# Projections ordered by mixer group, loads that wait for their own group's stores, and attention woven in from inside the first projection

## The chip, the cores and the metric

The kernel runs on one core of a Trainium2 chip. The metric is the device time of one execution in microseconds (us). The engines are called as in the profile: PE is TensorE (matmuls), PEld its weight loads, DVE is VectorE, ACT is ScalarE, POOL is GpSimd, SP is SyncE.

## The reference

One inference step of a two-layer encoder (model width 1024) for two request groups: a prompt of 1024 new frames, and 32 next frames of a running stream with 512 cached ones. All is float32. In each layer:

```python
u = rmsnorm(x, norm1) @ w_in          # one projection, its columns cut into
# A: aq, ak, av (6 heads)   B: bq, bk, bv (5 heads), index iq, ik, iw   C: cq, cf, ci, cg (5 heads)
oa = diff_attend(aq, ak, av)          # softmax(q1 k1) - lam * softmax(q2 k2), chunk-causal
ob = dsa_attend(bq, iq, iw, bk, bv, ik)   # keys picked by top-256 of an index score, then softmax
oc = hgrn2(cq, cf, ci)                # gated linear recurrence
x = x + concat(rms(oa), ob, rms(oc) * silu(cg)) @ w_out
x = x + (silu(conv3(h @ up_a)) * (h @ up_g)) @ w_down      # h = rmsnorm(x, norm2)
```

Rotated keys, values, index keys, the recurrence's states and the convolution's tails are outputs too.

## The kernel before, in words

**Passes.** The 1056 frames are cut into two halves: half 0 is the first 512 prompt frames and the 32 running ones (544 columns, in column groups of 272 and 272), half 1 the other 512 (groups of 256). A layer and a half are a pass, and `PROJS` numbers them: pass 0 is layer 0, half 0; pass 1 is layer 0, half 1; passes 2 and 3 the same in layer 1.

**Dense work** is a list of 974 turns (`TURNS`), in stages in this order: P00, P01, F00, P10, F01, P11, F10, Y0, F11, Y1, where P is a projection, F the output projection with the FFN, Y the last norm, and the digits are layer and half. A turn is one accumulated group of matmuls, eight as a rule, and each of them leaves two records in the trace, so a turn has 16. The kinds:
- `f`: one 128-row tile of the transposed projection (weights stationary, L650). 19 tiles `n`, two column groups `j` each. Two tiles x = 0, 1 make a bundle of mixer B (n 0 to 7) or A (n 8 to 13), whose halves POOL rotates (rotary embedding); each of n 14 to 18 is a bundle of mixer C. ScalarE evicts the turn into `ub` (L917), POOL rotates into `tb` (L1540 to L1545), SP stores to `projT` in HBM. Both buffers hold two bundles.
- `t`: values and gates with frames as rows (frames stationary, L658), six chunks `p` of 224 weight columns. A chunk has one turn for each unit of 128 frames (and one for the 32 running ones), so five in half 0 and four in half 1. Evicted into `tout` (two buffers, L923), stored to `projN`.
- `wo`, `a`, `g`, `dn`: output projection, the FFN's two up-projections and its down-projection, all on L650. `nsq` and `nsc`: a norm's mean by matmul (L627) of squares that ScalarE makes (L899), then ScalarE's square root (L904), VectorE's reciprocal and its products `xn`.

In numbers of turns P00 is 0 to 71 and P01 72 to 137. Weights come through a ring of three tiles; SP loads a tile when the third before it is done. On SP's one queue stand, in the order of turns, the weight loads, the bundles' stores (taken up four turns after a bundle's last turn) and the `t` stores (one turn after).

**Mixer work** is a list of steps: per pass X (index scores and picks, steps `load`, `dots`, `near`, `far`, `pick`), B (attention of mixers B and A: a load step, one step for each item and three to drain), C (HGRN2: three head pairs of ten steps), M (merge). An item is one head and one unit of frames. Its scores (L713 for B, L728 for A) go to PSUM; VectorE masks and takes maxima (L1313 for B), ScalarE takes exponentials (L1038), VectorE scales them (L1324), TensorE transposes (L744), ScalarE copies (L1050), TensorE multiplies by values (L761, L768), ScalarE copies out (L1061, L1064). In C, step 7 makes products of pairs (L795), which VectorE masks and sums and ScalarE copies (L1137), and step 8 uses them (L863, L864).

**The order of both** is written out ahead of time. `weave` gives one string of "d" (next dense turn) and "s" (next step), and PE, ACT and DVE all follow it. A step may not stand before its turn `first`. For X that is turn 5's tile plus LAG = 6; for B, C and M it is the end of the pass's whole projection plus 6:

```python
first = LAST["f", l, h, 5, 0] + 1 + LAG if kind == "X" else STAGE["P%d%d" % (l, h)][1] + LAG
while j < len(steps) and i >= steps[j][0] and y / need <= (x + time / 2) / have:
```

Steps are shared out by their estimated times: `y` counts step time given out and `x` dense time passed, and when `first` is late, all steps that are due by then come at once. That happens in pass 0, where turns 22 to 137 (P00 and P01) share X, B, C and M of pass 0: X ends behind turn 53, and behind turn 77 stand 37 steps of B in a row; the other 22 stand behind turns 78 to 93. In pass 2 the same 59 steps are spread behind turns 428 to 487 in F01. In the scalar engine's program (`att_scalar`) the B part begins with a wait for all stores of the pass's projection, and then `load_pair` issues the loads of the first two head pairs (7 DMAs each in half 0).

## Time and profile before

| | |
|---|---|
| median of three runs | 4173.93 us (4170.97 to 4179.95) |
| the profiled execution's own time | 4175.74 us |
| its span, first to last instruction | 4173.9 us |
| mean granted TensorE clock | 0.945 |
| TensorE busy | 3863.0 us (93%) |
| VectorE, ScalarE, POOL busy | 54%, 26%, 15% |
| HBM traffic | 80 GB/s over the span |

Busy time of PE is the union of pipelined matmuls, so it says whether the engine had work and not how fast it went; the granted clock tells which of its two levels, 1.2 or 2.4 GHz, it had, as a mean over a stretch (0.5 is all at 1.2 GHz). The page cuts the span into 40 slices of 104 us and gives busy shares and the granted clock in tenths. A row of the timeline gives an instruction or several merged ones with start and duration, and in brackets the idle time of the engine before it and what ended it. Line numbers are those of the kernel before.

### The profile page before, as it was taken

The numbers are of one execution on the slowest core, as the hardware profiler recorded it, in microseconds if no ns is written. First come the engines' busy times: TensorE is split into PE (matmuls) and PEld (weight loads), VectorE is DVE, ScalarE is ACT, GpSimd is POOL, SyncE is SP. The second block draws the span as 40 slices with busy tenths as digits, with TensorE's granted clock in tenths as the row PEclk, the third lists the DMA queues.
The fourth block names the chain that finished last, engine by engine and source line by source line (L and its number), as shares of the span: only waits on it lengthen the run. The fifth ranks groups of instructions, "written<-read, shape, count | busy, mean of one in ns | idle before, by whom it ended". The sixth has DMA issues, their size and how long they took to land.

```text
span 4173.9 us, 54852 instructions
## 1 busy us (share of the span) xinstructions
PE 3863.0 (93%) x22040; PEld 3134.7 (75%) x22040; DVE 2243.5 (54%) x4588; ACT 1083.9 (26%) x2674; POOL 645.0 (15%) x732
## 2 busy tenths in 40 slices
PE   7996889999999999999999998999999999799997
PEld 6773667877876777887767776897767777688886
DVE  1744654599954564449555553489835564521112
ACT  1113333211124342221333232111144433211111
POOL 3200230211001133020000014302000101421013
PEclk9995898999999999999999999999999998899999
DMA  3321222322122122232221113333211211332222
GB/s 129 116 77 59 62 69 89 107 86 71 55 85 66 57 85 88 89 111 91 77 87 54 59 56 105 109 115 104 67 57 54 74 39 57 103 121 71 71 75 93
DMA packets 152565, 338.04 MB, mean 81 GB/s; under 512 B 30312, under 2 KB 70760, under 8 KB 141048
## 3 DMA queue, kind: packets, MB, share of 16 engines
q1 hardware_dynamic: 91800, 289.52, 22.1%
q10 hardware_dynamic: 60512, 45.02, 3.8%
q8 instruction: 175, 2.87, 0.3%
q14 instruction: 78, 0.64, 0.1%
HBM read 298.34 MB, written 36.14 MB: 80 GB/s over the span
## 4 chain that ended last, share of the span: by engine, by line
PE 71%; DVE 18%; DMA 3%; ACT 3%; ACTq 2%; issue 2%; POOL 1%; SPq 0%; DVEq 0%; POOLq 0%
PE PS L650 48%; PE PS L658 7%; DVE scr L1285 5%; DVE top L1284 4%; PE PS L744 3%; PE PS L728 3%; PE PS L768 2%; PE PS L761 2%; PE PS L713 1%; DMA out_projT<-dense 1%; PE PS L864 1%; PE PS L863 1%; PE PS L795 1%; DVE xn L1231 1%; DMA iw<-out_projT 1%
## 5 line engine op out<-in xcount | busy, mean ns | idle before, releaser
L650 PE MATMUL PS<-xn,wring 128*128 128x272 f32 (+1 forms) x8064 | 1883.3, 394 | 48.1 <-ACT dense L940 19.9
L650 PEld LDWEIGHTS PS<-xn,wring 128*128 128x128 f32 x8064 | 1551.8, 194 | 335.3 <-issue 38.8
L1512 POOL TENSOR_TENSOR xT<-xT,res 128x272 f32<-128x272 f32 (+1 forms) x320 | 254.2, 795 | 2810.6 <-ACT res L909 2765.4
L650 PE MATMUL PS<-dense,wring 128*128 128x256 f32 (+1 forms) x2816 | 668.5, 396 | 16.3 <-ACT res L909 7.9
L650 PEld LDWEIGHTS PS<-dense,wring 128*128 128x128 f32 x2816 | 540.9, 195 | 116.9 <-issue 14.3
L1284 DVE MAX8 top<-scr 128x8 f32<-128x384 f32 (+6 forms) x418 | 367.5, 879 | 12.5
L1285 DVE MATCH_REPLACE8 scr<-top,scr 128x384 f32<-128x384 f32 (+6 forms) x418 | 359.8, 861 | 0.0
L658 PE MATMUL PS<-wring,xn 128*128 128x224 f32 (+1 forms) x1728 | 352.2, 365 | 6.0 <-ACT dense L923 6.0
L658 PEld LDWEIGHTS PS<-wring,xn 128*128 128x128 f32 (+1 forms) x1728 | 319.1, 188 | 32.0 <-issue 9.5
L909 ACT ACTIVATE res<-PS 128x272 f32<-128x272 f32 (+1 forms) x320 | 124.2, 389 | 640.5 <-PE PS L650 617.8
L650 PE MATMUL PS<-catT,wring 128*128 128x272 f32 (+1 forms) x1024 | 235.5, 392 | 7.5 <-DMA wring<-in_wo 6.9
L650 PEld LDWEIGHTS PS<-catT,wring 128*128 128x128 f32 x1024 | 196.4, 193 | 46.2 <-DMA wring<-in_wo 7.3
L744 PE MATMUL PS<-ident,scr 128*128 128x128 f32 (+1 forms) x902 | 165.9, 294 | 63.3 <-ACT scr L1050 44.6
L744 PEld LDWEIGHTS PS<-ident,scr 128*128 128x128 f32 (+1 forms) x902 | 104.5, 151 | 155.2 <-issue 54.7
L1313 DVE CUSTOM_DVE_ANT_0 scr<-PS,bias 128x128 f32<-128x128 f32 (+8 forms) x90 | 67.7, 753 | 255.9 <-PE PS L744 235.9
L938 ACT ACTIVATE dense<-PS 128x256 f32<-128x256 f32 (+1 forms) x176 | 68.6, 391 | 475.8 <-PE PS L650 468.2
L1050 ACT ACTIVATE scr<-PS 128x512 f32<-128x512 f32 (+4 forms) x308 | 139.1, 452 | 186.3 <-PE PS L744 133.1
L1303 DVE MEMSET PS<- 64x64 f32 x192 | 21.5, 112 | 308.1 <-PE PS L728 307.6
L1305 DVE TENSOR_REDUCE mx<-PS 128x1 f32<-128x640 f32 (+6 forms) x216 | 162.5, 752 | 31.8 <-PE PS L728 25.3
L917 ACT ACTIVATE dense<-PS 128x256 f32<-128x256 f32 (+1 forms) x152 | 58.6, 389 | 444.3 <-PE PS L650 330.7
L1038 ACT ACTIVATE scr<-PS,ngm 128x640 f32<-128x640 f32 (+6 forms) x216 | 157.4, 731 | 43.2 <-DVE ngm L1306 42.7
L728 PE MATMUL PS<-kv 32*128 32x512 f32 (+5 forms) x672 | 140.0, 524 | 23.5 <-ACT scr L1038 20.2
(172 smaller groups left out, 3343.1 us busy)
## 6 DMA issues: line engine op xcount, KB each, us to landing
wring<-in_wu SPq DMA_DIRECT2D x88, 1024.0 KB, 4.9
wring<-in_wf SPq DMA_DIRECT2D x76, 512.0 KB, 3.8
wring<-in_wo SPq DMA_DIRECT2D x64, 512.0 KB, 3.6
wring<-in_wd SPq DMA_DIRECT2D x96, 320.0 KB, 2.9
wring<-in_wd SPq DMA_DIRECT2D x64, 384.0 KB, 3.1
wring<-in_wn SPq DMA_DIRECT2D x24, 896.0 KB, 5.0
kv<-out_projT ACTq DMA_DIRECT2D x48, 256.0 KB, 3.9
out_projN<-dense SPq DMA_DIRECT2D x96, 112.0 KB, 1.7
```

The lines of the kernel that those rows point to most:

```text
L650: mm = nc.tensor.matmul(PS[:, dbank(t.g0), 0:cw], wtile(t.q, i), rhs, start=(kk == a), stop=(kk == b - 1))
L658: mm = nc.tensor.matmul(PS[:u.w, dbank(t.g0), 0:CW], xn[:, kk, u.col:u.col + u.w], wtile(t.q, kk, CW), start=(kk == 0), stop=(kk == KD - 1))
L728: mm = nc.tensor.matmul(PS[:u.w, abank(s, u, x) + a // 512, 0:b - a], q[r, u.col:u.col + u.w], k[r, u.key + a:u.key + b], start=True, stop ...
L744: tr = nc.tensor.transpose(PS[:kw, 4, (kt % 4) * P:(kt % 4) * P + u.w], soft(s, 0)[:u.w, kt * P:kt * P + kw], ident[:u.w, :u.w])
L761: mm = nc.tensor.matmul(PS[r0:r0 + D, 5, 0:u.w], v[:kw, u.vt + kt, D * it.hh:D * it.hh + D], pt_of(it)[:kw, kt, 0:u.w], start=(kt == 0), s ...
L909: nc.scalar.activation(res[:, i % NRES, 0:cw], PS[:, dbank(t.g0), 0:cw], ACT.Copy).then_inc(s_ea, 1)
L1038: nc.scalar.activation(dst, src, ACT.Exp, bias=ngm[:u.w, s % 4, x:x + 1], scale=scale_a if g == "a" else 1.0, accum_out=sums[:u.w, s % 4, ...
L1050: nc.scalar.activation(pt_of(items[s])[:kw, 4 * z:4 * z + n, 0:u.w], src[:, :, 0:u.w], ACT.Copy).then_inc(s_pc, 1)
L1284: step(nc.vector.max(top[:u.w, :], wk))
L1285: step(nc.vector.match_replace(wk, top[:u.w, :], wk, SENTINEL))
L1305: step(nc.vector.tensor_reduce(mx[:u.w, i, x:x + 1], sc, AX, ALU.max))
L1512: nc.gpsimd.tensor_tensor(x, x, res[:, i % NRES, 0:cw], ALU.add).then_inc(s_res, 1)
```

## The change

- `SECTIONS` orders the turns of each projection by mixer: section b is f tiles 0 to 7 and then t chunks 1, 2, 3; section a is f tiles 8 to 13 and chunk 0; section c is f tiles 14 to 18 and chunks 4, 5. Turns and their number are the same.
- Each `load_pair` waits for the stores of its own section and those before it, in place of one wait for all.
- `weave` lets a B step start six turns after the end of the section whose loads it needs (`step_groups`), and C and M after section c. Shares are counted as a running credit.
- The squares of tiles 5 to 7 of a layer-0 norm go to a free part of `cat`, since `catT` 5 to 7 may hold attention's output by then.

```diff
--- before.py
+++ after.py
@@ -59,6 +59,8 @@
 C_AV, C_BV, C_CI, C_CG, WN = 0, 384, 704, 1024, 1344
 NCH, CW = 6, 224
 
+SECTIONS = (("b", 8, (1, 2, 3)), ("a", 14, (0,)), ("c", NPT, (4, 5)))
+
 P_N1, P_N2, P_CONV, P_HIST, P_AG, P_CG, P_LI, PCOLS = 0, 8, 16, 104, 148, 212, 276, 278
 
 LEVELS = (64, 32, 16, 8, 4, 2)
@@ -93,13 +95,17 @@
 
     if l == 0:
         _norm(l, h, 0, 0, 1)
-    for n, j in ((0, 0), (1, 0), (2, 0), (0, 1), (1, 1), (2, 1)) + tuple((n, j) for n in range(3, NPT) for j in range(2)):
-        _turn("f", l, h, n, 0, j, load=("f", l, h, n, 0))
-        if (n, j) == (0, 0):
-            _norm(l, h, 0, 1, 1 - l)
-    for p in range(NCH):
-        for u in UNITS[h]:
-            _turn("t", l, h, u.slot, p, load=("t", l, h, 0, p))
+    order = ((0, 0), (1, 0), (2, 0), (0, 1), (1, 1), (2, 1)) + tuple((n, j) for n in range(3, NPT) for j in range(2))
+    done = 0
+    for g, end, chunks in SECTIONS:
+        for n, j in order[2 * done:2 * end]:
+            _turn("f", l, h, n, 0, j, load=("f", l, h, n, 0))
+            if (n, j) == (0, 0):
+                _norm(l, h, 0, 1, 1 - l)
+        for p in chunks:
+            for u in UNITS[h]:
+                _turn("t", l, h, u.slot, p, load=("t", l, h, 0, p))
+        done = end
 
 
 def _added(kind, l, h, p, norm):
@@ -155,6 +161,17 @@
 
 ADDS = {k: i for i, k in enumerate([k for k, t in enumerate(TURNS) if t.kind in ("wo", "dn")])}
 T_COUNT = {m: sum(1 for t in TURNS if t.kind == "t" and PROJS.index((t.l, t.h)) <= m) for m in range(4)}
+
+
+def section_end(m, g):
+
+    l, h = PROJS[m]
+    return LAST["t", l, h, UNITS[h][-1].slot, [x for x in SECTIONS if x[0] == g][0][2][-1]] + 1
+
+
+
+T_SECTION = {(m, g): sum(1 for t in TURNS[:section_end(m, g)] if t.kind == "t") for m in range(4) for g in "abc"}
+B_SECTION = {g: max(r for r, x in enumerate(BUNDLES) if x[0] == g) for g in "abc"}
 
 
 def groups_done(name):
@@ -296,24 +313,46 @@
 LAG = 6
 
 
+def step_groups(m):
+
+    items = ITEMS[m]
+    firsts = sorted({it.first for it in items})
+    out = ["b"]
+    for s in range(len(items) + 3):
+        g = items[min(s, len(items) - 1)].g
+        if s - 3 in firsts and s > 3:
+            g = max(g, "bac"[(firsts.index(s - 3) + 1) // 3], key="bac".index)
+        out.append(g)
+    return out
+
+
 def weave(dense, mixers):
+
 
     steps = []
     for kind, m in mixers:
         l, h = PROJS[m]
-        first = LAST["f", l, h, 5, 0] + 1 + LAG if kind == "X" else STAGE["P%d%d" % (l, h)][1] + LAG
-        if m and kind != "X":
-            first = max(first, STAGE["F%d%d" % PROJS[m - 1]][0] + 2 * KD + 2)
-        for pe, act, dve, wait in step_times(kind, m):
+        for i, (pe, act, dve, wait) in enumerate(step_times(kind, m)):
+            if kind == "X":
+                first = LAST["f", l, h, 5, 0] + 1 + LAG
+            else:
+                first = section_end(m, step_groups(m)[i] if kind == "B" else "c") + LAG
+                if m:
+                    first = max(first, STAGE["F%d%d" % PROJS[m - 1]][0] + 2 * KD + 2)
             steps.append((first, 0.3 + max(wait, act + dve if kind in "CM" else max(act, dve))))
     turns = [(i, turn_time(TURNS[i])) for i in dense]
     have, need = sum(t for i, t in turns), sum(max(0.2, t) for first, t in steps) or 1
-    plan, j, x, y = "", 0, 0.0, 0.0
+    plan, j, credit = "", 0, 0.0
     for i, time in turns:
-        while j < len(steps) and i >= steps[j][0] and y / need <= (x + time / 2) / have:
-            y += max(0.2, steps[j][1])
+        credit += time / 2 * need / max(have, 1)
+        while j < len(steps) and i >= steps[j][0] and credit >= 0:
+            t = max(0.2, steps[j][1])
+            credit, need = credit - t, need - t
             plan, j = plan + "s", j + 1
-        plan, x = plan + "d", x + time
+        if j < len(steps) and i < steps[j][0]:
+            credit = min(credit, 0.0)
+        plan, have = plan + "d", have - time
+        credit += time / 2 * need / max(have, 1)
     return plan + "s" * (len(steps) - j)
 
 
@@ -489,6 +528,10 @@
 
 
         obank = (5, 0)
+
+        def square_of(kk, c, cw):
+
+            return catT[:, kk, c:c + cw] if kk < 5 else cat[:, kk - 5, C_CAT:C_CAT + cw]
 
 
         def idx_views(h):
@@ -624,7 +667,7 @@
                     if t.p:
                         for kk in range(KD):
                             pe.wait_ge(s_sq, KD * norms_before(k) + kk + 1)
-                            mm = nc.tensor.matmul(out, mean[:], catT[:, kk, c:c + cw], start=(kk == 0), stop=(kk == KD - 1))
+                            mm = nc.tensor.matmul(out, mean[:], square_of(kk, c, cw), start=(kk == 0), stop=(kk == KD - 1))
                     else:
                         pe.wait_ge(s_acc, norms_before(k) - 4 + 1)
                         mm = nc.tensor.matmul(out, mean[:], xn[:, SUM, c:c + cw], start=True, stop=True)
@@ -896,7 +939,7 @@
                 if t.kind == "nsq" and t.p:
                     for kk in range(KD):
                         act.wait_ge(s_x[t.h][kk], 16)
-                        nc.scalar.activation(catT[:, kk, c:c + cw], xT[:, kk, xcols(t.h, c, cw)], ACT.Square).then_inc(s_sq, 1)
+                        nc.scalar.activation(square_of(kk, c, cw), xT[:, kk, xcols(t.h, c, cw)], ACT.Square).then_inc(s_sq, 1)
                 elif t.kind == "nsc":
                     z = TURNS[k - 1]
                     act.wait_ge(s_xn, KD * (norms_before(k) - 1))
@@ -955,6 +998,11 @@
             q, k, v = q_of(jj), k_of(jj), v_of(jj)
             rq, rk, cv = {"a": (R_AQ, R_AK, C_AV), "b": (R_BQ, R_BK, C_BV), "c": (R_CQ, R_CF, C_CI)}[g]
             rq, rk, cv = rq + P * pair, rk + P * pair, cv + P * pair
+
+            for i in range(2):
+                act.wait_ge(s_st[i], max(stored(m, r) for r in range(B_SECTION[g] + 1) if (m * NB + r) % 2 == i))
+            for i in range(NTO):
+                act.wait_ge(s_to[i], 16 * len([x for x in range(T_SECTION[m, g]) if x % NTO == i]))
             now = slice(C0[h], C0[h] + W[h])
             tiles = lambda a: projN[l, a:a + HALF, cv:cv + pw].rearrange("(i p) c -> p i c", p=P)
             act.eng.dma_start(q[:pw, 0:W[h]], projT[l, rq:rq + pw, now]).then_inc(s, 16)
@@ -1063,10 +1111,6 @@
                 c = (2 * pair + hh) * D
                 nc.scalar.activation(cat[:u.w, u.slot, c:c + D], PS[:u.w, 5, 0:D], ACT.Copy).then_inc(s_o, 1)
 
-            for i in range(2):
-                act.wait_ge(s_st[i], max(stored(m, r) for r in range(NB) if (m * NB + r) % 2 == i))
-            for i in range(NTO):
-                act.wait_ge(s_to[i], 16 * len([x for x in range(T_COUNT[m]) if x % NTO == i]))
             if m:
                 act.wait_ge(s_ct, CT_COUNT[m - 1])
             load_pair(act, m, 0)
```

Where it moves instructions. In P00 `X` ends behind turn 54 and B begins behind turn 55; 32 of its steps stand in P00, two or three to a turn, and from step 37 on they stand where they stood. The first place is PE at the end of P00 and the start of P01. Before, the t turns (x8 is one turn) run on into the norms of pass 1, and all of the first scores and transposes follow the second f turn behind them:

```order
L658 MATMUL PS<-wring,xn 128x224 x32
L658 MATMUL PS<-wring,xn 32x224 x8
L627 MATMUL PS<-catT,mean 128x256 x8
L650 MATMUL PS<-xn,wring 128x256 x8
L627 MATMUL PS<-catT,mean 128x256 x8
L650 MATMUL PS<-xn,wring 128x256 x8
L713 MATMUL PS<-kv 128x128 x2
L713 MATMUL PS<-kv 128x256 x2
L744 MATMUL PS<-ident,scr 128x128 x2
L713 MATMUL PS<-kv 128x384 x2
```

Now, from f turn 52 on (L693 is L650 of before, L756 is L713, L787 is L744, L804 is L761):

```order
L693 MATMUL PS<-xn,wring 128x272 x48
L756 MATMUL PS<-kv 128x128 x2
L756 MATMUL PS<-kv 128x256 x2
L787 MATMUL PS<-ident,scr 128x128
L693 MATMUL PS<-xn,wring 128x272 x8
L787 MATMUL PS<-ident,scr 128x128
L756 MATMUL PS<-kv 128x384 x2
L787 MATMUL PS<-ident,scr 128x128 x2
L804 MATMUL PS<-scr,kv 64x128 x2
L787 MATMUL PS<-ident,scr 128x128 x2
L693 MATMUL PS<-xn,wring 128x272 x8
L756 MATMUL PS<-kv 128x512 x2
```

So the first scores moved from behind turn 77 to behind turn 57, with a dense turn after every two or three steps.

The second place is ACT at the first norm of pass 1. Before, it stands between the evictions of t and f turns, ahead of all attention:

```order
L923 ACTIVATE dense<-PS 32x224
L899 ACTIVATE catT<-xT 128x256 x8
L904 ACTIVATE inv<-PS,epst 128x256
L917 ACTIVATE dense<-PS 128x256
L899 ACTIVATE catT<-xT 128x256 x8
L904 ACTIVATE inv<-PS,epst 128x256
L917 ACTIVATE dense<-PS 128x256
L960 DMA kv<-out_projT 128x544
```

Now (L942 is L899, L947 is L904, L1086 the exponentials of L1038, L1098 the copies of L1050, L1112 those of L1064):

```order
L1086 ACTIVATE scr,sums<-PS,ngm 128x128 x2
L942 ACTIVATE catT<-xT 128x256 x5
L942 ACTIVATE cat<-xT 128x256 x3
L1112 ACTIVATE cat<-PS 128x64
L1098 ACTIVATE scr<-PS 128x4x32
L1098 ACTIVATE scr<-PS 32x32
L1086 ACTIVATE scr,sums<-PS,ngm 128x256 x2
L947 ACT_TABLE_LOAD
L947 ACTIVATE inv<-PS,epst 128x256
L1112 ACTIVATE cat<-PS 32x64
L1098 ACTIVATE scr<-PS 128x128
L1086 ACT_TABLE_LOAD
```

One step's exponentials now stand between a norm's squares and its root, and the tables of the two functions alternate. In mixer C the step before and the step after the products change places with turns as follows: in pass 0, step 7 stood behind turns 103, 114 and 127 and step 8 behind 104, 116 and 128; they stand now behind 104, 116, 127 and 106, 117, 129. In pass 1 it was 336, 351, 368 and 338, 353, 370, and is 338, 354, 369 and 340, 355, 370, where 353 and 370 were t turns and 354 to 356 and 369, 370 are f turns.

## Rows read from the trace of the kernel before

**Rows 1.** The page: busy time of each engine, and the clock in 40 slices

```profile
PE 3863.0 (93%) x22040; PEld 3134.7 (75%) x22040; DVE 2243.5 (54%) x4588; ACT 1083.9 (26%) x2674; POOL 645.0 (15%) x732
...
PEclk9995898999999999999999999999999998899999
```

**Rows 2.** Busy time by stretch, all engines (columns in the first line)

```profile
core 0: us, PE busy (x) PEld busy (x) DVE busy (x) ACT busy (x) POOL busy (x), PEclk, DMA share, GB/s
315.40:446.70 131.30, 87.59 (x405) 51.30 (x405) 59.40 (x232) 46.61 (x153) 0.00 (x0) 0.54 0.16 47
2005.00:2166.80 161.80, 148.72 (x829) 111.42 (x827) 72.11 (x254) 58.62 (x187) 11.62 (x16) 0.97 0.25 80
220.00:296.00 76.00, 75.75 (x384) 66.70 (x384) 26.66 (x54) 8.60 (x25) 0.00 (x0) 0.98 0.23 73
446.70:562.00 115.30, 102.83 (x553) 77.44 (x553) 66.61 (x188) 40.33 (x145) 31.41 (x24) 0.93 0.25 75
```

**Rows 3.** The same by stretch for line L650 alone

```profile
315.40:446.70 131.30, 0.02 (x1) 0.12 (x1) 0.54 0.16 47
446.70:562.00 115.30, 64.11 (x257) 50.98 (x257) 0.93 0.25 75
2005.00:2166.80 161.80, 100.75 (x425) 79.74 (x423) 0.97 0.25 80
```

**Rows 4.** Waits from 315.4 to 446.7 us: total, times, longest

```profile
DVE scr L1313 <- PE PS L744: 41.3, 23, 4.3
ACT catT L1061 <- PE PS L761: 34.4, 15, 3.6
...
PE PS L728 <- ACT scr L1038: 13.4, 5, 5.5
```

**Rows 5.** The chain that ended last: start, us, what (two unbroken runs)

```profile
1129.04 60.75 PE PS L650 x264
...
3697.79 418.13 PE PS L650 x1936
```

**Rows 6.** Timeline of DVE: end of pass 0's picks

```profile
247.53 0.43 DVE L1287 TENSOR_SCALAR bias<-scr 32x544 f32<-32x544 f32 x1
```

**Rows 7.** Timeline of PE: its wait before turn 48

```profile
220.24 6.08 PE L658 MATMUL PS<-wring,xn 128*128 128x224 f32 x23 [5.22 <-ACT dense L923]
```

**Rows 8.** Timeline of PE: the norm of pass 1, and the first scores

```profile
303.59 3.69 PE L650 MATMUL PS<-xn,wring 128*128 128x256 f32 x16 [3.02 <-DVE xn L1231]
...
322.67 1.65 PE L713 MATMUL PS<-kv 64*128 64x128 f32 x8 [7.31 <-DMA kv<-out_projN]
```

**Rows 9.** Timeline of ACT: a norm's root among pass 1's exponentials

```profile
1483.37 1.28 ACT L904 ACT_TABLE_LOAD   x1
1484.66 0.49 ACT L904 ACTIVATE inv<-PS,epst 128x272 f32<-128x272 f32 x1
...
1490.05 1.28 ACT L1038 ACT_TABLE_LOAD   x1
```

**Rows 10.** Timeline of PE: starts of mixer C's step 8, passes 0 and 1

```profile
618.41 1.09 PE L864 MATMUL PS<-kv,bias 128*128 128x64 f32 x4 [6.22 <-ACT bias L1137]
...
689.58 0.63 PE L864 MATMUL PS<-kv,bias 128*128 128x64 f32 x4 [2.11 <-ACT bias L1137]
...
743.82 0.41 PE L864 MATMUL PS<-kv,bias 128*128 128x64 f32 x2 [1.44 <-ACT bias L1137]
...
1644.14 0.40 PE L863 MATMUL PS<-carry,bias 64*128 64x64 f32 x2 [2.11 <-issue]
...
1717.79 0.40 PE L863 MATMUL PS<-carry,bias 64*128 64x64 f32 x2 [2.01 <-issue]
...
1787.77 0.40 PE L863 MATMUL PS<-carry,bias 64*128 64x64 f32 x2 [1.25 <-issue]
```

**Rows 11.** Waits over the span: evictions of f turns for stores

```profile
ACT dense L917 <- DMA out_projT<-dense: 106.9, 21, 10.0
```

**Rows 12.** Timeline of POOL: first of six instructions of a rotation

```profile
96.72 1.34 POOL L1540 TENSOR_TENSOR dense<-dense 128x544 f32<-128x544 f32 x1 [6.27 <-ACT dense L917]
```

**Rows 13.** The page: the largest tile's load, KB, us to landing

```profile
wring<-in_wn SPq DMA_DIRECT2D x24, 896.0 KB, 5.0
```

## The prediction

> **What bounds the kernel now.** I read the page's shares first. TensorE is busy for 93% of the span, VectorE for 54%, ScalarE for 26%, and the granted clock is full nearly everywhere except in the fourth and fifth slice, where it reads 5 and 8 [rows 1]. So TensorE is the bound, and what is to be had lies where it idles or runs at its lower level. The second view is the table by stretches. From 315.4 to 446.7 us TensorE holds 87.6 of 131.3 us at a granted clock of 0.54, almost all of it at 1.2 GHz [rows 2]; in that stretch VectorE is busy for 59.4 us and ScalarE for 46.6, so none of the three is full. The same stretch counted for the dense line alone shows one matmul record, the tail of a turn [rows 3]. It is the place where the plan puts 37 steps of the first attention (mixer B of pass 0: the load step and items 0 to 35) behind one dense turn, because all loads of attention waited for the end of the first projection plus six turns. The waits there form a ring between TensorE, ScalarE and VectorE, none over 8 us [rows 4]: a chain of latencies with nothing to put under it.
>
> **Part 1: the 37 steps move under dense turns.** The change starts them 22 turns earlier, two or three to a turn, and leaves the total of dense work as it is. What the same steps cost when woven is in this trace: the attention of pass 2 (layer 1, same half, same items) has them from 2005.0 to 2166.8 us. Both stretches hold the same 404 attention records: 405 less 1, and 829 less 425 [rows 2, 3]. A steady dense record of 256 columns takes 418.13 / 1936 = 0.216 us [rows 5], so 425 of them are 91.8 us of those 161.8, and attention adds 70.0 us. The gain by this is 131.3 - 70.0 = **61.3 us**. Two things make the new place less roomy. The dense work under the steps is about 66 us there (six turns of 16 records of 272 columns at 60.75 / 264 = 0.230 us, ten turns of 16 records of 224 at 75.75 / 384 = 0.197, two norms' and two more turns' worth of 256) instead of 91.8 [rows 2, 5]. TensorE idle was 43.7 us with no cover and 161.8 - 148.7 = 13.1 with 91.8 [rows 2]; on a line between them, 66 us of cover leave 21.7, or 8.6 more. Against this, in pass 2 VectorE also carries the FFN's convolutions, which are absent here. I take half, 4.3. The gain is 57.0. Its best case is that only TensorE's own attention work remains: 148.7 - 91.8 = 56.9 us, a gain of 74.4. Its worst near row is pass 0's own tail: steps 37 to 58 fill 115.3 us with 257 dense records (55.5 us), so 59.8 us for 22 steps or 2.72 each [rows 2, 3]; 36 such are 97.9, a gain of 33.4.
>
> Can the steps start there? VectorE must have finished the index picks. The last of them ends at 248.0 us [rows 6]. TensorE stands at turn 48 until 220.24 us [rows 7], since ScalarE's next ReLU, behind turn 45, waits for VectorE's picks. In the new order that step sits behind turn 47, and the turns from 20 on before it are 15 t, 12 f and one more t (94.7 us) where they were 22 f and 4 t (93.6); so TensorE resumes at about the same time. Two t and six f turns, 28 us, are left before the first attention step, which it reaches at 248. That is level with the picks' end: a wait of 0 to 5 us, and I take 0 since the first scores need only the loads. The loads (14 DMAs on ScalarE's queue) wait now for the stores of their own section, whose last turn is 20 turns back. Their flight is exposed for 7.3 us today [rows 8]; two f turns now lie over it. Its rest stands in pass 2's 70.0 too.
>
> **Part 2: the norm inside attention.** Pass 1's first norm was alone on ScalarE; TensorE lost 3.02 us between its mean and the first turn after it [rows 8]. Now its square roots stand among exponentials. Where that happens already, ScalarE loads a table of 1.28 us before the root and another before the next exponential [rows 9]; so four loads are added, 5.1 us of ScalarE, of which the two before the roots are on the path to xn (2.6 us), and the exponentials of one step queue ahead of each root (up to 2 x 0.6). I charge **+5 us**, bounds 0 and +10.
> The Trainium skill (ScalarE: Activation LUTs, "What ACT_TABLE_LOAD costs" and "Table sets: the hidden batching unit") speaks against this edit: do all of one set before switching, for each switch is a load of about 1.28 us plus a drain of 1.38. By it the four switches would be 10.6 us and not 5.1, and this term would be estimated at +10. The trace agrees on the load but not on the drain, as the root starts 1.29 us after its load does [rows 9].
>
> **Part 3: t turns between f turns in all four projections.** The count of turns is unchanged, so dense work is too. What shifts is what lies between mixer C's step 7 and step 8, where TensorE waits for VectorE and ScalarE. These waits are 6.2, 2.1 and 1.4 us in pass 0, and 2.1, 2.0 and 1.3 in pass 1 [rows 10]. The plan gives pass 0 one f turn more of cover in the first pair (3.4 us), one t turn less in the second (-3.0), 3.9 more in the third; so 3.4 and 1.4 are saved and 3.0 lost, -1.8. Pass 1 loses 1.3, 2.4 and 2.4, so +6.1. Sum **+4 us**, bounds -8 (the 9.8 us of pass 0's waits shrink to 2) and +15 (each of the six grows by 2.5). Passes 2 and 3 have C beside the FFN, with the same plan to within a turn: 0. The index load of passes 0 and 3 now flies under three t turns in place of two or three f turns: 1 us either way, 0.
> The stores: ScalarE waits 106.9 us in 21 waits for stores of f bundles to leave their buffer [rows 11], mostly under TensorE's two banks. A section boundary gives the stores 15 or 5 t turns to drain, which can only help, but the runs of f turns inside a section have the same rhythm; 0, at best -8. On SP's queue a bundle's store now stands among t stores: POOL needs 6 x 1.34 us for the rotation [rows 12], and SP takes it up four turns later, 12.6 us of t turns, so nothing behind it is held. A weight tile is in use for two f turns (7 us) or four or five t turns and lands 5.0 us after its issue where it is longest [rows 13]: 0.
> Squares of three of the eight tiles go to another buffer: same instructions, 0.
>
> **Sum.** -57.0 + 5 + 4 = -48 us. Against the profiled span of 4173.9 us that is 4126. The profiled run itself took 4175.7 us and the median is 4173.9, so the sum stands for the median too: **4126 us**.
>
> **The rivals.**
> *Thin cover costs nothing* (chance 0.15). Only TensorE's own work remains: -74.4 + 5 + 4 = -65, 4109 us. For it: VectorE and ScalarE are half idle in the stretch. Against: even in pass 2 TensorE idles 13.1 us.
> *A crowded weave* (0.16). Steps cost what pass 0's tail shows, 2.72 us each, because ScalarE's in-order queue holds evictions, stores' waits and exponentials together: -33.4 + 9 = -24, 4150 us. For it: the tail is the same pass beside f turns. Against: the sections used are c and t, with lighter stores.
> *The low clock spreads* (0.04, the slower side). With three short steps to a turn, TensorE's small matmuls and gaps keep the clock at 1.2 GHz from turn 57 to 77. The steps then cost the 131.3 us they cost now, and the 66 us of dense work under them take 132: +66 + 9 = +75, 4249 us. It decides below a mean clock of about (66 + 56.9) / (131.3 + 66) = 0.62 in that stretch. For it: 0.54 in today's burst. Against: 0.97 in pass 2 with up to two steps to a turn.
> *It doesn't take hold* (0.03). The early steps are queued but VectorE or the loads hold TensorE at the first of them, so that the stretch of dense turns is spent before attention flows: a change within 8 us.
>
> **How the numbers follow.** My forecast has 0.62, and its own range is 4112 to 4140: the cover term between 0 and 8.6, the norm between 0 and 10, mixer C between 0 and 9. The range 4100 to 4152 takes in the better rival and the crowded weave's centre, and leaves out the tails of these two and the last two. A measurement here can tell about 0.2%, 8 us, from no change. Faster by more: 0.62 + 0.15 + 0.16 = 0.93; within it 0.03; slower 0.04.
>
> **What would show it.** In the profile after: no stretch without dense records after turn 77; the granted clock of the fourth slice at 9; the attention records of the 37 steps between about 247 and 400 us, with TensorE idle near 15 to 22 us there; table loads from three to five at the exponentials' line and from four to six at the root's; C's waits before step 8 moved as said. The prediction is wrong if the clock in that stretch stays under 0.8, if TensorE waits over 10 us at the first scores, if the second projection's dense turns come more than 10 us apart from what they do now, or if another stage moves by over 10 us.

## The result, and the profile after

| | before | after |
|---|---|---|
| median (4 runs each) | 4175.74 us | 4138.89 us |
| lowest to highest | 4170.97 to 4179.95 | 4134.61 to 4142.42 |
| ratio, 95% interval | | 0.9912 [0.9894, 0.9929] |
| profiled execution, its span | 4175.7, 4173.9 | 4142.4, 4140.2 |

The change makes the kernel 36.8 us faster; 48 were forecast (4126), and the measured time lies inside the range. The sign and the range held. The sum held less well than that sounds, as the stages show. A stage's time runs here from its first dense record to the next stage's:

| stage | before | after | moved | forecast |
|---|---|---|---|---|
| P00 and P01 | 771.5 | 745.7 | -25.7 | -53.8 |
| F00 | 717.3 | 716.6 | -0.7 | 0 |
| P10 | 324.3 | 337.0 | +12.7 | +6.1 |
| F01 | 738.6 | 729.4 | -9.2 | 0 |
| P11 | 225.3 | 223.7 | -1.6 | 0 |
| F10 | 830.8 | 821.1 | -9.7 | 0 |
| F11 | 533.5 | 533.9 | +0.4 | 0 |

The stages are those of the two profiled executions, and their moves add to -33.8 us. The first stages gave half of what was forecast, and two later ones gave 19 us that no term had.

The page of the changed kernel, busy time and granted clock, to be read beside [rows 1]:

```profile
PE 3837.9 (93%) x22040; PEld 3123.8 (75%) x22040; DVE 2245.1 (54%) x4588; ACT 1088.2 (26%) x2678; POOL 644.5 (16%) x732
...
PEclk9998898999999999999999998999999999899999
```

TensorE is busy for 25 us less with the same 22040 records, so most of the gain is clock and not idle time. In P00 and P01 it is 12.5 us less of busy time and 13.2 us less of idle time. The fourth slice, 5 before, reads 8, where 9 was forecast; the fifth stays 8.

The attention that stood in the burst, by stretch (columns as in [rows 2]), from its first scores (turn 57) to turn 77, and from there to mixer C's start:

```profile
243.90:404.50 160.60, 127.71 (x679) 90.85 (x678) 59.29 (x223) 58.23 (x182) 0.00 (x0) 0.87 0.27 82
404.50:542.80 138.30, 118.27 (x573) 90.04 (x572) 75.49 (x213) 45.54 (x154) 31.35 (x24) 0.84 0.21 68
```

The first stretch by groups of instructions on TensorE (dense lines L693 and L701, norm L670, the rest attention; then busy, mean ns of one, idle before):

```profile
L701 PE MATMUL PS<-wring,xn 128*128 128x224 f32 (+1 forms) x160 | 41.0, 421 | 0.0
L693 PE MATMUL PS<-xn,wring 128*128 128x272 f32 (+1 forms) x97 | 26.7, 434 | 3.3 <-DVE xn L1275 3.3
L787 PE MATMUL PS<-ident,scr 128*128 128x128 f32 (+2 forms) x96 | 17.7, 282 | 15.7 <-ACT scr L1098 8.1 <-DVE scr L1368 7.4 <-DVE scr L1375 0.2
...
L756 PE MATMUL PS<-kv 64*128 64x128 f32 (+5 forms) x60 | 12.7, 449 | 5.1 <-DVE ngm L1359 3.0 <-DMA kv<-out_projN 2.1
L771 PE MATMUL PS<-kv 32*128 32x128 f32 (+5 forms) x48 | 9.4, 487 | 4.1 <-ACT scr L1086 4.1
```

TensorE idles 160.6 - 127.7 = 32.9 us in it. Of these, 8.0 are waits at the norm's lines (4.7 at L670 and 3.3 at L693), which belong to part 2 of the forecast. And the ten t turns, 160 records, take 41.0 us; at the steady 0.197 us a record [rows 2] they are 31.5. Such a loss was in no term of the sum: the granted clock is 0.87, between the two levels, so part of the work ran at the lower one.

All steps that stood in the burst are through at 419.6 us, the end of the steps behind turn 77. From turn 57 to there:

```profile
243.86:419.60 175.74, 136.37 (x727) 97.92 (x725) 71.61 (x259) 65.53 (x200) 0.00 (x0) 0.86 0.24 75
```

TensorE idles 39.4 us in it, and 14.2 of them are the waits at the two norms that are counted below. That leaves 25.2 us for the steps themselves; the forecast had 21.7 on its line and 17.4 after its allowance of 4.3.

The norm of pass 1, TensorE's timeline and then VectorE's (start, us):

```profile
404.50 3.67 PE L693 MATMUL PS<-xn,wring 128*128 128x256 f32 x16
...
409.73 0.70 PE L771 MATMUL PS<-kv 32*128 32x256 f32 x4
416.42 0.63 PE L787 MATMUL PS<-ident,scr 32*128 32x32 f32 x4 [5.99 <-DVE scr L1375]
```

```profile
408.49 1.75 DVE L1270 RECIPROCAL inv<-inv 128x256 f32<-128x256 f32 x1 [1.39 <-ACT inv L947]
410.27 3.26 DVE L1275 SCALAR_TENSOR_TENSOR xn<-xT,par,inv 128x256 f32<-128x256 f32 x8
413.54 0.11 DVE L1347 MEMSET PS<- 64x64 f32 x1
...
415.60 0.77 DVE L1375 SCALAR_TENSOR_TENSOR scr<-scr,rs 32x544 f32<-32x544 f32 x1
```

Attention's transposes wait 5.99 us. VectorE first stands 1.39 us for ScalarE's root; then the second norm's reciprocal and products, 5.0 us on VectorE, stand in its queue ahead of the row maxima and the combining of two attention maps. All waits at the two norms, from 375.7 to 419.6 us:

```profile
PE PS L787 <- DVE scr L1375: 6.2, 2, 6.0
PE PS L670 <- ACT catT L942: 4.7, 2, 2.9
PE PS L693 <- DVE xn L1275: 3.3, 1, 3.3
```

That is 14.2 us where the same norms cost 4.8 before (3.0 of it in [rows 8]): +9.4, against a charge of 5. What P00 and P01 take over their dense records at steady rates (0.216, 0.230 and 0.197 us by width) divides as follows:

| turns, steps | before | after | moved |
|---|---|---|---|
| all ahead of the burst's steps (to turn 76, to turn 56) | 41.7 | 34.1 | -7.6 |
| the burst's 37 steps (turn 77; turns 57 to 77) | 131.5 | 112.0 | -19.5 |
| the rest of B (turns 78 to 94) | 61.4 | 69.4 | +8.0 |
| C and the merge (turns 95 to 137) | 81.3 | 74.6 | -6.7 |

The norms' waits stand in the first row before (4.8) and in the second after (14.2). Without them the burst's steps cost 131.5 and 97.8.

### The profile page after: what moved, and what is told of

It reads as the page before. It is cut to its first block, busy times and chain, and to the rows that moved or that the text cites. A ratio compares the mean times of both kernels' runs of the same rounds, so it can differ in the third digit from the quotient of the medians.

```text
span 4140.2 us, 54858 instructions
## 1 busy us (share of the span) xinstructions
PE 3837.9 (93%) x22040; PEld 3123.8 (75%) x22040; DVE 2245.1 (54%) x4588; ACT 1088.2 (26%) x2678; POOL 644.5 (16%) x732
## 4 chain that ended last, share of the span: by engine, by line
PE 74%; DVE 16%; ACT 3%; DMA 2%; issue 2%; ACTq 2%; POOL 0%; SPq 0%; DVEq 0%; POOLq 0%
PE PS L693 52%; PE PS L701 6%; DVE scr L1329 5%; DVE top L1328 4%; PE PS L787 3%; PE PS L771 3%; PE PS L811 2%; PE PS L804 1%; PE PS L756 1%; PE PS L907 1%; PE PS L838 1%; PE PS L906 1%; DMA out_projT<-dense 1%; DVE xn L1275 1%; ACT scr L1098 1%
## 5 line engine op out<-in xcount | busy, mean ns | idle before, releaser
L693 PE MATMUL PS<-xn,wring 128*128 128x272 f32 (+1 forms) x8064 | 1886.3, 394 | 52.2 <-ACT dense L983 24.4
L693 PEld LDWEIGHTS PS<-xn,wring 128*128 128x128 f32 x8064 | 1552.9, 194 | 338.8 <-issue 35.5
L693 PE MATMUL PS<-dense,wring 128*128 128x256 f32 (+1 forms) x2816 | 669.9, 396 | 15.3 <-DVE dense L1260 6.5
L693 PEld LDWEIGHTS PS<-dense,wring 128*128 128x128 f32 x2816 | 542.4, 195 | 115.5 <-issue 10.7
L701 PE MATMUL PS<-wring,xn 128*128 128x224 f32 (+1 forms) x1728 | 365.1, 372 | 16.1 <-ACT dense L966 12.9
L1328 DVE MAX8 top<-scr 128x8 f32<-128x384 f32 (+6 forms) x418 | 367.5, 879 | 12.5
L701 PEld LDWEIGHTS PS<-wring,xn 128*128 128x128 f32 (+1 forms) x1728 | 326.0, 192 | 44.5 <-issue 14.2
L693 PE MATMUL PS<-catT,wring 128*128 128x272 f32 (+1 forms) x1024 | 234.2, 390 | 9.3 <-DMA wring<-in_wo 8.7
L693 PEld LDWEIGHTS PS<-catT,wring 128*128 128x128 f32 x1024 | 195.5, 192 | 47.5 <-DMA wring<-in_wo 9.1
L787 PE MATMUL PS<-ident,scr 128*128 128x128 f32 (+1 forms) x902 | 157.9, 283 | 69.8 <-ACT scr L1098 45.4
L787 PEld LDWEIGHTS PS<-ident,scr 128*128 128x128 f32 (+1 forms) x902 | 100.1, 145 | 152.0 <-issue 53.9
L1098 ACT ACTIVATE scr<-PS 128x512 f32<-128x512 f32 (+4 forms) x308 | 139.0, 451 | 180.0 <-PE PS L787 126.5
L1086 ACT ACTIVATE scr<-PS,ngm 128x640 f32<-128x640 f32 (+6 forms) x216 | 157.3, 730 | 45.5 <-DVE ngm L1350 45.0
L1584 POOL TENSOR_TENSOR dense<-dense 128x544 f32<-128x544 f32 (+3 forms) x28 | 37.5, 1341 | 810.7 <-ACT dense L960 767.6
## 6 DMA issues: line engine op xcount, KB each, us to landing
out_projN<-dense SPq DMA_DIRECT2D x96, 112.0 KB, 1.7
```

What stands on the lines that cost most here:

```text
L693: mm = nc.tensor.matmul(PS[:, dbank(t.g0), 0:cw], wtile(t.q, i), rhs, start=(kk == a), stop=(kk == b - 1))
L701: mm = nc.tensor.matmul(PS[:u.w, dbank(t.g0), 0:CW], xn[:, kk, u.col:u.col + u.w], wtile(t.q, kk, CW), start=(kk == 0), stop=(kk == KD - 1))
L787: tr = nc.tensor.transpose(PS[:kw, 4, (kt % 4) * P:(kt % 4) * P + u.w], soft(s, 0)[:u.w, kt * P:kt * P + kw], ident[:u.w, :u.w])
L1086: nc.scalar.activation(dst, src, ACT.Exp, bias=ngm[:u.w, s % 4, x:x + 1], scale=scale_a if g == "a" else 1.0, accum_out=sums[:u.w, s % 4, ...
L1098: nc.scalar.activation(pt_of(items[s])[:kw, 4 * z:4 * z + n, 0:u.w], src[:, :, 0:u.w], ACT.Copy).then_inc(s_pc, 1)
L1328: step(nc.vector.max(top[:u.w, :], wk))
```

## The experiments

All twelve kernels were timed in five rounds beside the kernel before; their medians are from 4 to 12 runs. The kernel before had 4172.4 us beside e1 to e4, 4170.8 beside e5 to e8, 4172.1 beside e9 and e10, and 4176.3 beside e11 and e12. Two theories stood after the result. By the first the gain is the **early start**. By the second, my own rival, it is the **sharing rule**, which the change rewrote too and whose own price the forecast never worked out: a share that falls due while steps are not allowed is no longer saved up, and that alone dissolves the burst. Where I compare stages I compare one profiled execution with another.

### The parts of the change

**e1**: the kernel before with `SECTIONS` and the new order of turns in a projection, nothing else.

```
-    for n, j in ((0, 0), (1, 0), (2, 0), (0, 1), (1, 1), (2, 1)) + tuple((n, j) for n in range(3, NPT) for j in range(2)):
+    for g, end, chunks in SECTIONS:
+        for n, j in order[2 * done:2 * end]:
...
+        for p in chunks:
```

> The kernel before with the new order of the projection turns alone (t turns between f turns by mixer group); where attention steps may start, and the rule that shares them out, are those of before. Early start theory (the gain is that 37 steps of mixer B of pass 0 can lie behind dense turns of P00): the burst of 37 steps stays where it was at the head of P01, so this kernel stays within 8 us of before, 4168 to 4184 us. Rival, order theory (f and t turns mixed are what relieves projections): at least 20 us below before, 4155 us or less. Also read: whether P10 is longer (337 us in the changed kernel against 324 before) and F01 and F10 shorter by 9 us each; if order does it, they are here.

Measured 4168.5 us, ratio 0.999 [0.9973, 1.0008]. Its burst is where it was. P10 322.6 us, F01 736.8, F10 822.8. The order alone does nothing to the time that can be told from noise. Inside it, P00 and P01 take 777.1 us, 5.6 more than before, and F10 takes 8.0 less.

**e2**: the kernel before with the changed loop in `weave`, nothing else.

```
-        while j < len(steps) and i >= steps[j][0] and y / need <= (x + time / 2) / have:
-            y += max(0.2, steps[j][1])
+        credit += time / 2 * need / max(have, 1)
+        while j < len(steps) and i >= steps[j][0] and credit >= 0:
+            t = max(0.2, steps[j][1])
+            credit, need = credit - t, need - t
...
```

> The kernel before with the new sharing rule alone: a share that came due while steps could not start is no longer saved up. So there is no burst: the 37 steps are spread over turns 6 to 33 of P01, at 2 to 3 steps a turn, and mixer C of pass 0 follows in turns 33 to 60. Early start theory: the cover of P01 alone is too thin for B and C together; of the burst's 131 us at most 15 come back, 4155 to 4180 us. Rival, rule theory (what cost was the burst, and any dense turn between steps hides most of it): the whole gain is here, 4132 to 4146 us, and P00 and P01 together end at about 764 us as in the changed kernel. P10, F01 and F10 as in the changed kernel if the rule moves them.

Measured 4184.0 us, ratio 1.0033 [1.0013, 1.0052]: slower, and above the ranges of both theories. The burst is gone (37 steps behind turns 77 to 91) and nothing is won. All engines from 315.7 to 479.0 us, and then its dense line (L655 here) alone:

```profile
315.70:479.00 163.30, 126.21 (x615) 88.89 (x613) 59.99 (x216) 50.07 (x161) 24.41 (x19) 0.78 0.23 70
```

```profile
315.70:479.00 163.30, 67.14 (x225) 52.68 (x223) 0.78 0.23 70
```

225 dense records of 0.216 us [rows 5] are 48.6 us and took 67.1. In the burst of before the clock is lower, 0.54 [rows 2], but no dense record stands in it. Spread out over too few turns, the steps still leave gaps, and now the dense records run at the lower clock too. What the steps win, 131.5 - 121.7 = 9.8 us for the 37, the denser remainder of B loses again: steps 37 to 58 cost 82 us over their dense turns where they cost 60.

**e3**: the changed kernel with mixer B held back to the end of the whole projection.

```
-                first = section_end(m, step_groups(m)[i] if kind == "B" else "c") + LAG
+                first = section_end(m, "c") + LAG
```

> The changed kernel, but mixer B's steps may start only when the whole projection is stored, as before; order and rule of the changed kernel are kept. 48 turns of P01 must cover B, C and the rest of pass 0. Early start theory: 15 to 35 us above the changed kernel, 4154 to 4175 us, with P00 back at 279 us and P01 near 500. Rule theory: within 8 us of the changed kernel, 4131 to 4147 us.

Measured 4192.0 us, ratio 1.0044 [1.0026, 1.0061], 53 us above the changed kernel. Without the early start the change is slower than before, even above the range of the early-start theory; P01 takes 514.3 us. With e2 this rules out the rule as the source of the gain.

**e4**: the changed kernel with the sharing formula of before (e2's diff the other way round).

> The changed kernel with the sharing formula of before: B may start in P00 as changed, but its share saved up until turn 56 comes as a run of steps there. Early start theory: the run at the first possible turn is short of cover, so part of the gain goes, but B lies in P00 and P01 both: 4140 to 4165 us. Rule theory: most of the gain is gone, 4165 to 4180 us. P10, F01 and F10 as before if the rule moves them.

Measured 4128.7 us, ratio 0.9897 [0.9867, 0.9926], 43.8 us below before. That is 11 us below the range that I gave the early-start theory: I had expected a saved-up share to come as a run of steps at turn 56, but none does: the selection's steps last to turn 54, and B's plan is that of the change to within a turn. So order and early start bring 44 us, near the 48 of the forecast, though by other parts. The intervals of e4 and of the change overlap, so that it isn't shown by the whole time that the new rule gives 10 us of it back. The stages say where to look. P10 takes 335.6 to 337.0 us in the three kernels with the rule (the change, e2, e3) and 317.4 to 324.8 in the eight others up to e9. In e4 (first row) and in the change, the last steps of pass 1's attention, over turns 321 to 326, read:

```profile
1516.50:1551.40 34.90, 32.84 (x178) 26.90 (x178) 15.12 (x25) 12.09 (x26) 11.14 (x9) 1.00 0.26 83
```

```profile
1522.00:1566.40 44.40, 37.85 (x181) 30.68 (x180) 13.43 (x26) 11.64 (x26) 12.89 (x10) 0.85 0.26 80
```

The rule puts three of these steps one turn later. TensorE idles 6.6 us and not 2.1, 4.6 of them in one wait for a copy of ScalarE (L1098), and its clock falls to 0.85.

### What cover is worth

**e5**: e4, but B's steps may start at turn 67 and not 56.

```
                 if m:
                     first = max(first, STAGE["F%d%d" % PROJS[m - 1]][0] + 2 * KD + 2)
+                else:
+                    first = max(first, 67)
```

> The kernel of run e4 (the change with the sharing formula of before), but the steps of mixer B of pass 0 may start only at turn 67 in place of 56: 26 of them then stand in a row behind turn 66, and the ten turns 57 to 66, which had 25 steps between them, cover nothing. Nothing else moves. Cover theory (what counts is how many dense turns lie among the steps, each filling one wait; the kernels so far give (131.5 - 102)/20 = 1.5 us a turn): 12 to 18 us above e4, 4141 to 4147 us. Price-by-step theory (my forecast's: a step under dense turns costs 1.9 us, one without 3.55): 26 times 1.65 = 43 us above e4, about 4170 us. Third: dense turns cover nothing here and another difference of the change brings the gain: 4129 us, as e4.

Measured 4160.6 us, ratio 0.9968 [0.9955, 0.9981], 32 above e4; 21 of them lie between turn 57 and F00 (537.1 us and 515.8), the others in stages with the same plan. The same 413 records of turns 57 to 66 and their steps, in e4 and then in e5:

```profile
243.40:335.10 91.70, 73.24 (x413) 50.19 (x411) 29.13 (x123) 31.60 (x97) 0.00 (x0) 0.90 0.34 104
```

```profile
247.50:363.00 115.50, 86.73 (x413) 57.18 (x411) 28.95 (x123) 31.94 (x97) 0.00 (x0) 0.68 0.27 83
```

Ten turns out from between the steps cost 23.8 us: 10.3 of TensorE idle, and 13.5 of the same records taking longer at a clock of 0.68. So a covering turn is worth 2.4 us here, more than half of it clock. For the whole time the expectation by turns (12 to 18) was too low, since it had only waits in it, and that by steps (43) too high.

**e9**: e4 with at most two steps behind a turn from 56 to 93: the same turns cover, spread more evenly.

```
+        room = j + most_steps(i)
-        while j < len(steps) and i >= steps[j][0] and y / need <= (x + time / 2) / have:
+        while j < min(room, len(steps)) and i >= steps[j][0] and y / need <= (x + time / 2) / have:
```

> The kernel of run e4, but at most two attention steps behind a turn from turn 56 to 93: turns 57 to 66 then hold 20 steps in place of 25, and turns 67 to 72 twelve in place of seven; start, end and the number of dense turns among the steps are the same. Cover theory (each dense turn among steps fills one gap, however many steps stand in that gap's row, and all these turns fill one already in e4): within 4 us of e4, 4125 to 4133 us. Rival, crowding theory (three steps in a row cost more each than two): 6 to 12 us below e4, 4117 to 4123 us, with TensorE idle less in 57 to 66 than it gains in 67 to 72.

Measured 4136.6 us, ratio 0.9917 [0.9898, 0.9936]. From turn 57 to F00 it takes 513.8 us and e4 515.8: no gain from the even spread beyond 2 us, as the cover theory says. Its time is 8 us above e4's all the same, and over the range of the cover theory. The intervals of the two overlap, and the 8 us lie in the stages from F00 to F10, where both kernels have the same plan, so I read nothing from them.

**e6**: e4 with the index selection's share counted at 0.7, which frees seven more turns for B.

```
-            steps.append((first, 0.3 + max(wait, act + dve if kind in "CM" else max(act, dve))))
+            steps.append((first, (0.7 if (kind, m) == ("X", 0) else 1) * (0.3 + max(wait, act + dve if kind in "CM" else max(act, dve)))))
```

> The kernel of run e4, but the share of the index selection (X of pass 0) is counted at 0.7 of its cost, so its 49 steps lie in turns 22 to 47 in place of 22 to 55 and mixer B's scores start at turn 50 in place of 57: seven more turns for B and C to lie among. Cover theory: 7 times 1.1 to 1.5 = 8 to 11 us below e4, 4117 to 4121 us. Rival, VectorE bounds this stretch (it is busy 110.65 us of the 134.0 from 102 to 236 us in e4, nearly all with the selection): the picks cannot go faster than some 20 us sooner, TensorE's dense turns wait for VectorE instead, and the time stays at 4126 to 4135 us.

Measured 4160.8 us, ratio 0.9967 [0.9953, 0.9981], 32 us above e4. Worse than the rival had it. TensorE's waits during the selection, e4 and then e6:

```profile
PE PS L696 <- ACT dense L961: 9.9, 2, 7.5
PE PS L715 <- DMA iw<-out_projT: 1.1, 1, 1.1
```

```profile
PE PS L688 <- ACT dense L955: 13.7, 1, 13.7
PE PS L715 <- DMA iw<-out_projT: 8.7, 1, 8.7
PE PS L688 <- ACT dense L961: 6.9, 1, 6.9
```

The last pick ends on VectorE no sooner (at 244.5 us in e4 and 248.7 in e6), but the steps' ReLUs stand earlier in ScalarE's queue and wait longer there for VectorE, in e4 and then in e6:

```profile
ACT scr L1033 <- DVE scr L1313: 19.5, 2, 12.6
```

```profile
ACT scr L1033 <- DVE scr L1313: 32.0, 2, 20.0
```

Behind them its evictions are held up, and TensorE stands still. Mixer B's first scores begin near 250 us in both kernels, in e4 behind turn 57 and in e6 behind turn 50. Seven turns are simply done later, and they buy little: B costs 170.1 us over its dense turns, with e4 at 174.8.

### The norm inside attention

**e7**: e4 with no attention step behind turns 72 to 77; the seven steps follow behind turn 78.

```
+def kept_clear(i):
+    return 73 <= i <= 78
...
+        clear = kept_clear(i)
-        while j < len(steps) and i >= steps[j][0] and y / need <= (x + time / 2) / have:
+        while j < len(steps) and i >= steps[j][0] and not clear and y / need <= (x + time / 2) / have:
```

> The kernel of run e4 with no attention step behind turns 72 to 77, pass 1's first norms; the seven steps that were there follow in a row behind turn 78. If the norms inside attention are what costs (TensorE waits of 14 us there against 5 us before, by the trace of the changed kernel), 9 us of waits go and six turns of cover at 1.5 us go too: within 5 us of e4. If cover counts more, up to 10 us slower than e4; if the norm's disturbance is larger than its own waits (its low clock, 0.79 from 369 to 426 us in e4), 5 to 10 us faster.

Measured 4137.3 us, ratio 0.9913 [0.9898, 0.9928]. From turn 57 to F00 517.1 us against e4's 515.8: an even trade. The wait for L1375's counterpart falls from 6.2 to 0.2 us, and what it saved went into uncovered steps. The whole time is 9 us above e4's with intervals that overlap, and the profiled execution is the slowest of its six; it exceeds e4's mainly ahead of turn 57 and in F00 and P10, where the plans are the same.

**e8**: e4 with the square root of pass 1's first two norms computed as an exponential; values behind it differ from there on.

```
-nc.scalar.activation(inv[:, c:c + cw], PS[:, dbank(z.g0), 0:cw], ACT.Sqrt, bias=epst[:]).then_inc(s_ea, 1)
+nc.scalar.activation(inv[:, c:c + cw], PS[:, dbank(z.g0), 0:cw], ACT.Exp if (t.l, t.h, t.n) == (0, 1, 0) else ACT.Sqrt, bias=epst[:]).then_inc(s_ea, 1)
```

> The kernel of run e4, in which the square root of pass 1's two first norms is computed as an exponential instead (this part of the computation is changed, and so all values behind it), so that ScalarE needs no other function table among the exponentials of attention: two loads to the root's table and two back to the exponentials' go. If ScalarE's table loads cost what the forecast charged, 1.28 us each on the path: 3 to 6 us below e4. If the waits at the norms are VectorE's (its norm work stands in its queue ahead of attention's): within 2 us of e4 in the stretch of P01's first turns, and TensorE's wait of 6 us for the negation of the maxima stays. Data-dependent work is none, so the rest of the kernel stays as in e4.

Measured 4126.3 us, ratio 0.989 [0.9877, 0.9903]. ScalarE's table loads at the exponentials' line are back from five to three and at the root's from six to four. Turn 57 to F00 takes 512.7 us, 3.1 less than in e4; the whole time is 2.4 us less, which is not clear of noise. Its waits at the norm, from 376.9 to 415 us and then from 415 to 424 us:

```profile
PE PS L665 <- ACT catT L937: 4.7, 2, 2.9
PE PS L688 <- DVE xn L1270: 1.9, 1, 1.9
```

```profile
PE PS L782 <- DVE scr L1370: 4.6, 1, 4.6
```

In e4 these three waits are 4.8, 3.3 and 6.2 us, 14.3 together, and here 11.2: again 3.1 less, about 1.5 at each of the two behind the root. So four loads of 1.28 us, 5.1 us of ScalarE, are worth some 3 us here, or 0.8 each. The longest wait stays, 4.6 of 6.0 us, as it is VectorE's.

### Mixer C's step 8

In e4 TensorE waits 22.0 us in six pieces for the ScalarE copy ahead of step 8, over the whole kernel, and another 14.2 us in six where no releaser shows, at the other first line of the same step.

**e10**: the chain between step 7 and step 8 told to the plan.

```
-               (2, 2.4 * w, 5.5 * w, 0), (2, 2.4 * w, 4 * w, 0), (1.5, 0, 4.5, 0), (3, 1.8, 0, 0), (0, 1, 0, 0)]
+               (2, 2.4 * w, 5.5 * w, 0), (2, 2.4 * w, 4 * w, 0), (1.5, 0, 10.0, 0), (3, 1.8, 0, 0), (0, 1, 0, 0)]
```

> The kernel of run e4, but step 7 of mixer C's ten is counted at 11.5 us of work on ScalarE and VectorE in place of 6.0 (the chain behind it took 9.1 us in e4, from 646.68 to 655.78), so step 8 comes three to five turns after it in place of one or two, in all passes; B and the other steps of C move up by a turn or two for it. If the waits for that chain are real costs (in e4 TensorE waits 22.0 us in 6 pieces for the ScalarE copy that ends it): 10 to 22 us below e4, 4107 to 4119 us, spread over all four passes. If the steps that move up wait as much more as step 8 waits less: within 4 us of e4.

Measured 4172.4 us, ratio 1.0 [0.9987, 1.0013]: the whole gain is gone, which neither theory had. The wait did fall, from 22.0 to 12.2 us. But a larger share for C moves all that comes before it. The selection of pass 0 waits more, as in e6: from 106 to 246 us

```profile
PE PS L696 <- ACT dense L961: 10.6, 1, 10.6
PE PS L715 <- DMA iw<-out_projT: 8.4, 1, 8.4
```

That is 19.0 us where e4 has 11.0, and P00 and P01 grow by 12.2. The larger part lies elsewhere: F00 takes 734.4 us and not 715.3, with 52 records moved into it, and P10 331.7 and not 317.4, with 50 fewer. TensorE idles 14 us more in the two, and the clock in P10 is 0.91 and not 0.96. What holds these stages up was not tried.

**e11**: e4, and only step 8 waits, for three turns behind step 7.

```
-        while j < len(steps) and i >= steps[j][0] and y / need <= (x + time / 2) / have:
+        while j < len(steps) and i >= steps[j][0] and not (chained[j] and i < last + 3) and y / need <= (x + time / 2) / have:
```

> The kernel of run e4, but step 8 of each ten of mixer C comes at least three turns after step 7; the share of no other step is changed (steps 9 and 10 follow right behind, up to two turns later than in e4). Run e10 reached such gaps by moving everything ahead of them too, and its index selection and its mixer B lost more than C won. If it was that shift alone that cost e10 its 44 us: TensorE's waits for the ScalarE copy ahead of step 8 fall from 22.0 us to under 6, and the time is 8 to 18 us below e4, 4111 to 4121 us. If a wait of C only moves to the next step, the head of the next round: within 4 us of e4.

Measured 4118.7 us, ratio 0.9871 [0.9852, 0.989], 10 us below e4, though the intervals of the two overlap. The two waits over the span:

```profile
PE PS L903 <- ACT bias L1177: 11.0, 6, 2.1
PE PS L902 <- issue: 10.9, 6, 2.1
```

They fell from 36.2 to 21.9 us together. The first alone fell from 22.0 to 11.0, where under 6 were expected: 1.3 to 2.1 us stay at each of the twelve. With two turns between, before had 2.11 and 2.01 us already [rows 10], so this rest doesn't fall with the distance and isn't the chain; what it is, no run shows. From turn 57 to F00 it takes 506.3 us, 9.5 less than e4.

**e12**: the changed kernel, its own rule kept, with the same hold.

```
-        while j < len(steps) and i >= steps[j][0] and credit >= 0:
+        while j < len(steps) and i >= steps[j][0] and not (chained[j] and i < last + 3) and credit >= 0:
```

> The changed kernel itself, its sharing rule kept, with the same hold on mixer C's step 8. The pair e12 and e11 stands as the changed kernel and e4 do: if the changed rule costs what its stages showed so far (P10 15 us longer, F01 9 us shorter, P00 and P01 4.5 to 12 us longer), e12 lies 6 to 14 us above e11, with P10 at 332 us or more against 322 or less. Against the changed kernel it is 5 to 15 us shorter if the hold is worth what e11 shows.

Measured 4118.9 us, ratio 0.9867 [0.9848, 0.9886]. It is 20 us below the changed kernel where 5 to 15 were expected, and the intervals of these two are apart, so the hold's gain is shown here. It is level with e11, where 6 to 14 above it were expected. P10 takes 326.0 us, and 332 or more were expected. So the rule has no fixed price. What it cost lay, by this, in where it happened to put steps. e11 and e12 beat both kernels; the two can't be told apart.

## Why the prediction was right, and where it was not

**The bound and the place: right.** The burst was the dearest place, and e3 shows that the early start of B is what pays: without it the rest of the change loses 20 us against before. Mixer B starts where it was forecast, at 247 us: TensorE waits 2.05 us there for the loads of the first scores (0 were forecast, up to 5 allowed).

**Part 1, -57.0 us: the term that failed.** The step is "on a line between them, 66 us of cover leave 21.7". Counted over its dense turns the 37 steps cost 131.5 us in the burst, and 112.0 in the change with the two norms inside. Without the norms' 14.2 that is 97.8, a gain of 33.7 where 57.0 were forecast. Of the 23.5 us between 97.8 and the forecast's 74.3, 7.8 are idle time (25.2 and not 17.4) and 15.7 are busy time over that of dense records at full clock (72.6 and not 56.9). So two things were wrong in it. Idle time: in pass 2, from which the price came, one or two steps follow a turn, and here two or three do, and by e9 a turn covers one gap however many steps stand behind it. And the clock, the larger part: the work was taken at its time in pass 2, at a clock of 0.97, though the trace of before showed 0.54 in the burst. That busy time grows with a lower clock e5 shows, where of 23.8 us for ten turns 13.5 are longer records. I had the clock only as a rival of all or nothing ("the low clock spreads"), and it came in part: 0.87 in the stretch, above the 0.62 where it would have turned the sign. The worst row of the working, pass 0's own tail with 33.4 us of gain, was nearly exact. The crowded weave, with 0.16, had this number; its reason, ScalarE's queue, was not tested, and e9 speaks against crowding as such.

**B's tail and C, not in the sum.** Steps 38 to 58 kept their places to within a turn and cost 69.4 us over dense turns 78 to 94, where steps 37 to 58 and C's first cost 61.4. The clock there is 0.86, against 0.92 before. e1 has the burst ahead of the same turns, as before, and costs 67.9 us at 0.87; so most of this came with the new order and not with the early start. The order gave about as much back in turns 95 to 137: 74.4 us in e1 and 74.6 in the change, against 81.3. The forecast had only part 3's waits for the order, and why the clock moved there stays open.

**Part 2, +5 us: too small, and the larger part elsewhere.** Waits at the norms rose by 9.4 us. Of the mechanism that was charged, the table switches, e8 gives some 3 us. Two waits that e8 leaves were not followed in the forecast: 4.6 us behind the norm in VectorE's queue, and the wait for the squares on ScalarE (L942), 4.7 us where it was 1.8. On the drain between two table sets (the Trainium skill, ScalarE: Activation LUTs, "What ACT_TABLE_LOAD costs") the changed kernel's trace speaks as that of before did. The root again starts 1.29 us after its load does:

```profile
382.93 1.28 ACT L947 ACT_TABLE_LOAD   x1
384.22 0.47 ACT L947 ACTIVATE inv<-PS,epst 128x256 f32<-128x256 f32 x1
```

By that page's 1.28 + 1.38 for each of four switches the term would be estimated at 10.6 us, near the 9.4 measured, but for another reason: e8 took all four away and got some 3.

**Part 3, +4 us: right for two passes, and nothing for all four.** The waits ahead of step 8 are 2.08, 5.92 and 1.26 us in pass 0, which is 0.5 less than before (forecast -1.8; the first fell and the second rose as said), and in pass 1 they grew from 5.4 to 10.0, +4.6 (forecast +6.1). But the order is not what moves them in pass 1: e1 has the t turns between the f turns, waits 6.5 us there, and its P10 is as short as before. With the sharing rule they are 8.3 (e2) and 10.0 us (e3), though e7, without it, has 8.6 by one longer wait. In the change's P10, TensorE also waits 4.6 us more for ScalarE's copies (L1098), and so the stage grew by 12.7 and not 6.1, over the 10 us that the forecast had named as a mark of being wrong. And passes 2 and 3 were put at 0 "to within a turn", where the turn counts: the rule puts one step 8 of each a turn later. In F01, before and after:

```profile
PE PS L864 <- ACT bias L1137: 11.7, 3, 5.5
```

```profile
PE PS L907 <- ACT bias L1181: 8.0, 3, 4.6
```

In F10 they fell from 7.7 to 6.1. Over all four passes the waits ahead of step 8 were 34.5 us and are 33.4.

**Passes 2 and 3, 0: -19 us in F01 and F10.** F01 is 729.4 to 730.8 us in the four kernels with the rule and 728.1 to 741.8 in the others; among those with the plan of before it is 730.4 in e8 and 741.8 in e9, so the stage's time alone doesn't show it. TensorE's idle time in it does: 47.8 to 51.2 us in the four, and 54.3 to 57.3 in the eight with the plan of before. So the rule saves some 3 to 9 us there, 3.7 of them in the change ahead of step 8. F10 moved by 9.7 us, and only 1.7 of them are idle time; the rest is busy time, at a clock of 0.96 against 0.95. The order moves 27 of its steps by one turn (e1, 822.8 us), but e2, with the order of before, has 825.4. Only the profile of before has 830.8. Whether that is the plan or scatter between executions stays open.

So -37 came from six tenths of part 1 and from two later stages that the sum had at 0, part of which may be scatter. That it came so near is partly luck. With the old rule (e4) it is -44, and P00 and P01 give only 30 of it.
